# Value weights of the memory attention as 512 columns of half the contraction, with one bank per token tile

## The reference

```python
def memory_attention(h, m, wq, wk, wv, wo):
    B, T, _ = h.shape
    M = m.shape[1]
    q = (h @ wq).reshape(B, T, MEM_HEADS, MEM_HEAD_DIM)
    k = (m @ wk).reshape(B, M, MEM_HEADS, MEM_HEAD_DIM)
    v = (m @ wv).reshape(B, M, MEM_HEADS, MEM_HEAD_DIM)
    ...
x = x + memory_attention(rmsnorm(x, ln2_g[l]), rmsnorm(mem, ln_mem_g[l]),
                         wq_mem[l], wk_mem[l], wv_mem[l], wo_mem[l])
```

## Time and profile before

| | us |
|---|---|
| median of 3 runs | 1462.21 (1461.76 to 1463.43) |
| the profiled execution | 1462.46 |
| its span | 1460.7 |
| TensorE busy in the span | 1396.7 |
| VectorE busy | 735.3 |
| ScalarE busy | 507.6 |
| mean granted TensorE clock | 0.991 |

### The profile page before, as it was taken

The page is one execution under the profiler, slowest core; times in us unless marked ns, Lnnn a source line. Parts: engine busy times, 40 slices in busy tenths (PEclk is TensorE's granted clock), DMA queues, the critical chain, the costliest instruction groups (busy, mean ns, idle before and its releaser), DMA issues.

```text
span 1460.7 us, 27620 instructions
## 1 busy us (share of the span) xinstructions
PE 1396.7 (96%) x11965; PEld 1066.0 (73%) x11965; DVE 735.3 (50%) x1294; ACT 507.6 (35%) x872; POOL 137.4 (9%) x271
## 2 busy tenths in 40 slices
PE   7999999999999999999999999999999999899996
PEld 7998989898999999997889988874343333333332
DVE  4684947666667555555464354562332332233225
ACT  5543434334365555454353353421111101111003
POOL 7010110202200000000000000021011011010100
PEclk9999999999999999999999999999999999999998
DMA  7633333242494454437546516678999999999995
GB/s 236 192 117 117 124 118 114 91 142 80 143 323 149 148 166 161 129 130 273 179 157 189 190 44 234 218 298 336 395 421 422 421 420 421 421 422 421 422 411 217
DMA packets 161360, 351.02 MB, mean 240 GB/s; under 512 B 13824, under 2 KB 111706, under 8 KB 138330
## 3 DMA queue, kind: packets, MB, share of 16 engines
q1 hardware_dynamic: 161242, 349.30, 65.0%
HBM read 347.18 MB, written 2.10 MB: 239 GB/s over the span
## 4 chain that ended last, share of the span: by engine, by line
PE 85%; DMA 7%; DVE 4%; issue 2%; ACT 2%; SPq 0%; POOL 0%; DVEq 0%; POOLq 0%; ACTq 0%
PE banks L926 21%; PE banks L1538 13%; PE banks L1334 12%; PE banks L921 8%; PE banks L1574 6%; DMA expert_unit<-in_moe_w_down_dram 6%; PE banks L1399 5%; PE banks L1616 4%; PE banks L1509 1%; PE banks L1423 1%; PE banks L1446 1%; PE banks L1106 1%; PE banks L1383 1%; PE banks L1345 1%; PE banks L1133 1%
## 5 line engine op out<-in xcount | busy, mean ns | idle before, releaser
L1538 PE MATMUL banks<-expert_unit,pair_entries 128*64 128x512 f32 x1024 | 239.5, 612 | 23.9 <-issue 23.0
L926 PE MATMUL banks<-hidden_lo_chunks,piece 128*128 128x256 f32 x920 | 259.8, 282 | 0.0
L1800 ACT CAST piece<-arena_fixed 128x1024 fp32r<-128x1024 f32 (+1 forms) x158 | 161.6, 1032 | 176.0 <-PE banks L926 133.9
L2232 DVE TENSOR_TENSOR piece<-arena_fixed,piece 128x1024 fp32r<-128x1024 f32 (+1 forms) x158 | 188.8, 1219 | 46.6 <-ACT piece L1800 46.3
L1538 PEld LDWEIGHTS banks<-expert_unit,pair_entries 128*64 128x64 f32 x1024 | 72.4, 139 | 162.5 <-issue 162.4
L926 PE MATMUL banks<-hidden_hi_high_chunks,piece 128*128 128x256 f32 x928 | 178.2, 290 | 1.5 <-DVE hidden_lo_chunks L2215 1.5
L926 PE MATMUL banks<-hidden_hi_low_chunks,piece 128*128 128x256 f32 x912 | 176.3, 291 | 0.5 <-DVE piece L2232 0.5
L926 PEld LDWEIGHTS banks<-hidden_lo_chunks,piece 128*128 128x128 f32 x920 | 175.7, 191 | 0.0
L2496 DVE TENSOR_TENSOR loop_split<-arena_fixed,loop_split 128x2048 fp32r<-128x2048 f32 x48 | 107.9, 2288 | 101.5 <-ACT loop_split L1969 101.5
L2755 DVE TENSOR_TENSOR arena_phases<-arena_phases,banks 128x512 f32<-128x512 f32 x128 | 81.8, 682 | 135.2 <-PE banks L1616 135.2
L926 PEld LDWEIGHTS banks<-hidden_hi_high_chunks,piece 128*128 128x128 f32 x928 | 144.0, 191 | 6.4 <-issue 2.2
(11 more groups left out here) (418 smaller groups left out, 2064.8 us busy)
## 6 DMA issues: line engine op xcount, KB each, us to landing
expert_unit<-in_moe_w_gate_dram SPq DMA_DIRECT2D x60, 1024.0 KB, 22.7
expert_unit<-in_moe_w_up_dram SPq DMA_DIRECT2D x60, 1024.0 KB, 25.0
expert_unit<-in_moe_w_down_dram SPq DMA_DIRECT2D x52, 1024.0 KB, 22.8
arena_fixed<-in_w_in_dram SPq DMA_DIRECT2D x22, 2048.0 KB, 8.9
arena_fixed<-in_wk_mem_dram SPq DMA_DIRECT2D x8, 2048.0 KB, 8.4
arena_fixed<-in_wv_mem_dram SPq DMA_DIRECT2D x8, 2048.0 KB, 8.5
arena_fixed<-in_w_out_dram SPq DMA_DIRECT2D x8, 2048.0 KB, 8.0
arena_fixed<-in_wq_mem_dram SPq DMA_DIRECT2D x8, 2048.0 KB, 8.3
```

The lines of the kernel that those rows point to most:

```text
L926: mm = pe.matmul(b[:, half * T:half * T + T], w(w_)[:, k % 8, :], hidden_x(x_, c), start=c + t == 0 and n > 0, stop=c == NC - 1 and t == 2 ...
L1538: mm = pe.matmul(bank[b][o, :].rearrange("p (g n) -> p g n", g=2), hs_pair[:, c, o], gate_up_unit(i(e))[:, :, c % (NC // 2), :], start=c = ...
L1800: nc.scalar.copy(piece_half(p, 0), raw_piece(p)).then_inc(piece_hi, 1)
L2232: V.tensor_tensor(piece_half(p, 1), raw_piece(p), piece_half(p, 0).bitcast(F32), ALU.subtract)\
```

## The change

The value units get another shape. A unit now holds 512 columns and half of the contraction (8 chunks), so that units 2m and 2m + 1 together give columns 512m to 512m + 511. A piece is two chunks of 512 columns. A product streams 512 columns and fills a whole bank: token tile 0 has bank 0, tile 1 has bank 1, over both units of a pair. The product with zeros is left out; the first product of each bank starts it. Every second k is empty for values, since one product does the columns of two. In a piece the order is tile 0, chunks 0 and 1, then tile 1, chunks 0 and 1. A new semaphore, `value_tile`, tells that tile 0 of a pair is complete; ScalarE copies the two banks in a function of its own, in the gap that holds the end of the pair's second unit, ahead of the rounding of the next piece.

```diff
+        value_tile = sem("mem_values_first_tile")
...
+        def value_unit(n, i):
+
+            m, half = divmod(i, 2)
+            cs = slice(NC // 2 * half, NC // 2 * half + NC // 2)
+            return (slot(n % 2).rearrange("p (c n) -> p c n", n=2 * UC),
+                    wvm[:, cs, 2 * UC * m:2 * UC * m + 2 * UC])
...
-            return piece_buffer(p)[:, part, :].rearrange("p (c n) -> p c n", n=UC if keys[n][0] in TOKMAJOR else P)
+            width = 2 * UC if keys[n][0] == "mv" else UC if keys[n][0] in TOKMAJOR else P
+            return piece_buffer(p)[:, part, :].rearrange("p (c n) -> p c n", n=width)
...
+                elif key[0] == "mv":
+                    dst, src = value_unit(n, key[1])
...
+            def value_product(n, i, r):
+
+                if r % 2:
+                    return
+                m, half = divmod(i, 2)
+                p, tt, c2 = 4 * n + r // 8, r % 8 // 4, r % 4 // 2
+                c = NC // 2 * half + 2 * (r // 8) + c2
+                if half == 0 and r in (0, 4):
+                    pe.wait_ge(*act_proj.at(("mv", 2 * m - 2 + tt) if m else ("mk", 6 + tt)))
+                if r % 8 == 0:
+                    pe.wait_ge(piece_lo, piece_turn(p))
+                for t, (x_, w_) in enumerate(PASSES):
+                    mm = pe.matmul(bank[tt][:, :], hidden_x(x_, c)[:, tt * P:tt * P + P], piece_half(p, w_)[:, c2, :],
+                                   start=c + t == 0, stop=c == NC - 1 and t == 2)
+                if r % 8 == 6:
+                    mm.then_inc(piece_read, 1)
+                elif half and r == 2 * NC - 6:
+                    mm.then_inc(value_tile, 1)
...
+                if key[0] == "mv":
+                    return value_product(n, key[1], r)
...
-                    elif key[0] == "mv":
-                        dst = vm[:, :, j * UC:j * UC + UC]
...
                 for p in range(old // 8, new // 8):
+                    n, i = divmod(p, 4)
+                    if keys[n][0] == "mv" and keys[n][1] % 2 and i == 3:
+                        values_out(n, keys[n][1] // 2)
                     if p + NPB < PIECES:
                         piece_rounded(p + NPB)
-                    if p % 4 == 3:
-                        copy_out(p // 4)
+                    if keys[n][0] != "mv" and i == 3:
+                        copy_out(n)
+
+            def values_out(n, m):
+                for tt in range(NT):
+                    act.wait_ge(*((piece_read, 4 * n + 4) if tt else (value_tile, m + 1)))
+                    nc.scalar.copy(vm[:, tt, 2 * UC * m:2 * UC * m + 2 * UC], bank[tt][:, :])\
+                        .then_inc(*act_proj.mark(("mv", 2 * m + tt)))
```

## The result

| | before | after |
|---|---|---|
| median of 10 runs each, us | 1461.59 | 1464.45 |
| ratio, 95% interval | | 1.0020 (1.0012 to 1.0027) |
| the profiled execution, us | 1462.46 | 1463.16 |
| its span, us | 1460.7 | 1461.4 |
| mean granted clock | 0.991 | 0.989 |

The changed kernel is slower by 0.20%, 2.9 us between the medians (1.8 to 3.9 by the interval). The forecast was 1.7 us more, 1463.9; that difference lies just under the interval. The profiled execution of after is the second fastest of its ten.

What follows compares the result with a forecast made beforehand. TensorE alone was taken to bound the stretch of the value products. −6.96 us of savings, +6.92 of waits and +1.70 of a clock fall gave +1.66, so 1463.9 us, with an 8-in-10 range of 1459.0 to 1467.5.

Steps and rivals of the forecast that it cites:

- The width: TensorE's value products: 384 of 512 columns instead of 768 of 256 save 5.12 us.
- The rule of the Trainium skill weighed ahead: Product starts: columns over 2.4 GHz plus about 2.5 ns, so the wider value products would save only 0.96 us.
- The products with zeros: Opening product of each value unit's bank: dropping it saves 0.23 us eight times, 1.84 us.
- The waits: TensorE waits for ScalarE's bank copies at three pair ends: 2.50, 1.14 and 3.28 us, 6.92 in all.
- The clock: TensorE's granted clock falls once for the two long waits, costing 1.70 us; bounds 0 and 3.4.
- a choice at 0.40: Chance given to the forecast case, one fall of TensorE's clock behind the waits, 1463.9 us.
- The sum: Whole kernel: −6.96 saved, +6.92 of waits, +1.70 of a clock fall, +1.66 us.
- The rival in which ScalarE is in time: At pair ends, ScalarE copies before TensorE asks, leaving only the saving: 1455.2 us; chance 0.10.
- The rivals of a double price: Value products: a wide one costs twice a narrow one, so width saves nothing: 1469.0 us; chance 0.05.
- a wait that grows into the next step: Pair ends: ScalarE, delayed by two copies, falls behind and TensorE waits again; 9.9 us of waits, 1466.9; chance 0.07.

Runs made afterwards that it cites:

- e1: The changed kernel with the gap list shifted so that pairs end behind values steps, just before the scores; 1455.46 us, ratio 0.9962 to the kernel before.
- e3: The changed kernel with each 512-wide value product made as two of 256, and the gap list shifted as in e1; 1459.63 us, ratio 0.9990.
- e6: The kernel before without the value units' products with zeros, the first product starting the bank; 1459.74 us, ratio 0.9991.
- e4: The changed kernel with the gap list shifted so that each pair ends one product group into a gap behind scores; 1472.70 us, ratio 1.0078.
- e8: The changed kernel with ScalarE copying tile 0 one gap earlier where it is complete by then; 1460.49 us, ratio 0.9996.
- e2: The changed kernel with each 512-wide value product made as two of 256; same loads, order, banks and waits; 1468.55 us, ratio 1.0047.
- e9: The changed kernel measured again without any edit, beside the kernel before; 1465.89 us, ratio 1.0028.
- e7: The changed kernel with the gap list shifted for the last pair end only, gap 41 longer and 42 to 47 shorter; 1460.67 us, ratio 0.9994.
- e5: The kernel before with only the shifted gap list of e1, a control; 1461.12 us, ratio 1.0000.

## Why the prediction was right, point by point

- **The width** was forecast at 5.12 us and measured at 4.2 (e1 against e3). This is the term that was sized worst. The rate is right: 39 products in 8.87 us at the end of after, 0.227 each. What is missing goes, for the most part, at the changes between kinds, which the forecast, taken from unbroken rows of one kind, left out. Fifteen wide products after scores, transposes and values took 3.52, 3.45 and 3.41 us instead of 3.40, where thirty narrow ones took 3.69, 3.60 and 3.59 and so lost only 0.09, nothing and nothing. That is 0.03 more at each of seven gaps behind scores, 0.05 at each of eight behind transposes and 0.01 behind values, some 0.7 us of the 0.96. The rule of the Trainium skill weighed ahead (TensorE: Matmul & The Clock Gate, the section on 56 ns against 53.3 ns), by which the term is an estimated 0.96 us, doesn't hold for these products: e1 and e3 measure 4.2.
- **The products with zeros** were forecast at 1.84 and are 1.76 (e6) and 1.77 (e3).
- **The waits** were forecast at 2.50, 1.14 and 3.28, in all 6.92. By the timeline they are 2.42, 1.05 and 3.16 (idle plus 0.27), 6.63. The place of each, and what ends it, are as read. Ending the pairs just ahead of the scores removes them (e1), ending them sooner behind the scores lengthens them (e4), and an earlier copy shortens them (e8). So this step is shown, not only argued.
- **The clock** was forecast to fall once, for 1.70. In both profiles of the changed kernel it fell once, behind the third wait, and never behind the short one. That the count came out is partly luck: it was a choice at 0.40, and nearly the same waits had two falls in e2. The price in after: the twelve products from 626.24 on would have ended their starts at 626.24 + 0.11 + 12 × 0.2267 = 629.07, and the next kind begins at 630.69, 1.62 us later. In TensorE's timeline, the starts of every third product are 1.28 apart and not 0.68:

```profile
627.07 0.63 PE L914 MATMUL banks<-piece,hidden_lo_chunks 128*128 128x512 f32 x1
...
628.35 0.63 PE L914 MATMUL banks<-piece,hidden_lo_chunks 128*128 128x512 f32 x1
...
630.69 1.05 PE L1329 MATMUL banks<-arena_phases 128*128 128x128 f32 x8
```

- **The sum** was +1.66; the stretch shows +2.35. The saving was sized 1.03 too high, waits and fall 0.37 too high, and the two errors cancel in part. In medians it is +2.9, with an interval that holds 2.35 but not 1.66; e9 has +4.1. Whether the rest is more falls in executions that weren't profiled, I can't say. That 1464.45 lies only 0.6 from 1463.9 is luck in part: the median of before also came out 0.6 under the one that the forecast started from.
- The rival in which ScalarE is in time has the time of e1's kernel; it takes a different list of gaps, not a faster ScalarE. The rivals of a double price and of a wait that grows into the next step had nothing in any run.

## What to carry to other kernels

When a wider product takes the whole accumulator bank, ask which bank the next group writes, and at what place of its program the other engine empties the last one. If that place stands behind work that itself waits for TensorE, the wait is as long as that chain, less the products that TensorE still has to do, and here it could be read to about a tenth of a microsecond from the trace of before. Here the list that interleaves the work decides: with the gaps' ends moved by four to twelve steps of k, so that each pair ends just ahead of the scores, the same change is worth −0.38% instead of +0.20%.

## What the runs showed of the hardware that I had not expected

- A fall of the clock can come behind an idle time of 2.13 us (e2) or 2.15 (e7), and fail to come behind 2.15 (after, e9) and 2.47 (e8). It never came behind 0.69 or 0.78. All six of 2.75 us and more had one. In the expert stage of before, 2.71 had none and 2.15 had one, so the length of the idle time alone doesn't decide. What does stays open.
- Its price isn't fixed: 1.62 us in after, some 1.5 in e7, 2.2 on the mean of e4's three, where the windows around the first and the third lack twice as much full-speed time as the one behind the second.
- Two profiled executions of one program can differ by over a microsecond before the part under study (the same scores start at 541.30 in before and at 543.65 in e5, whose program is the same up to there, and at 539.92 and 539.71 in the two profiles of the changed kernel). A stretch with both ends in the same profile came out within 0.03 us of its counterpart, in e5 against before and in e9 against after.
